# A two-block transformer kernel on one core: seven instead of five FFN slab pairs by the seven-product scheme

## The reference

```
h   = rmsnorm(x, ffn_norm_g)                      # 256 x 2048
hid = h @ w_ffn_in                                # 2048 -> 2 * 5632
x   = x + (silu(hid[:, :5632]) * hid[:, 5632:]) @ w_ffn_out   # 5632 -> 2048
x   = x + sigmoid(rmsnorm(x, ple_norm_g) @ w_ple_gate) * (p @ w_ple)
```

## Time and profile before

| | |
|---|---|
| median of 3 runs | 2035.05 us (2034.72 to 2035.17) |
| the profiled execution's own time | 2034.51 us |
| its span in the trace | 2032.8 us |
| TensorE busy | 2016.9 us (99%) |
| VectorE busy | 1406.7 us (69%) |
| ScalarE busy | 1049.3 us (52%) |
| granted TensorE clock | 1.00 throughout |
| HBM read | 384.46 MB, 190 GB/s over the span |

### The profile page before, as it was taken

How to read it: one execution, slowest core, us unless ns; L and a number is a source line. 1 busy time by engine, 2 the same in 40 slices (tenths; PEclk the granted TensorE clock), 3 DMA queues, 4 the chain that set the end, 5 groups by cost and what they waited for, 6 DMA issues and landing times.

```text
span 2032.8 us, 23614 instructions
## 1 busy us (share of the span) xinstructions
PE 2016.9 (99%) x9325; PEld 1677.2 (83%) x9325; DVE 1406.7 (69%) x1488; ACT 1049.3 (52%) x1309; POOL 34.0 (2%) x44
## 2 busy tenths in 40 slices
PE   8999999999999999999999999999999999999999
PEld 7888888888888888888888887888888888888787
DVE  6877676555666665655554557888878888888764
ACT  6545444554465556544444445555555555555453
POOL 1000000000001100000000000000000000000000
PEclk9999999999999999999999999999999999999999
DMA  8545354555556544555555556676666756665553
GB/s 283 167 144 166 124 187 149 196 186 201 194 186 208 174 165 143 187 184 188 186 191 195 186 187 212 195 241 206 217 210 214 238 196 217 209 215 200 176 183 124
DMA packets 197721, 387.98 MB, mean 191 GB/s; under 512 B 9282, under 2 KB 10996, under 8 KB 197492
## 3 DMA queue, kind: packets, MB, share of 16 engines
q1 hardware_dynamic: 197620, 386.59, 56.9%
HBM read 384.46 MB, written 2.10 MB: 190 GB/s over the span
## 4 chain that ended last, share of the span: by engine, by line
PE 96%; DVE 2%; ACT 1%; issue 1%; DMA 0%; SPq 0%; ACTq 0%; DVEq 0%
PE acc L1099 54%; PE acc L1104 27%; PE aux L1498 6%; PE aux L1502 3%; PE aux L1082 2%; PE aux L1163 1%; DVE wlo L1588 1%; PE aux L1519 0%; ACT whi L709 0%; DMA resid<-in_x 0%; DVE actB_lo L2327 0%; DVE act_whole L2309 0%; PE aux L1153 0%; PE aux L1178 0%; DVE att_z L2088 0%
## 5 line engine op out<-in xcount | busy, mean ns | idle before, releaser
L1588 DVE TENSOR_TENSOR wlo<-raw,whi 128x1024 fp32r<-128x1024 f32 x624 | 761.3, 1224 | 542.8 <-ACT whi L709 537.6
L709 ACT ACTIVATE whi<-raw 128x1024 fp32r<-128x1024 f32 x624 | 659.1, 1060 | 863.9 <-PE acc L1104 810.8
L1099 PE MATMUL acc<-whi,actA_hi 128*128 128x512 f32 x1152 | 454.6, 395 | 1.7 <-DVE actA_lo L1603 1.2
L1099 PE MATMUL acc<-whi,actA_lo 128*128 128x512 f32 x1152 | 449.5, 390 | 0.0
L1099 PE MATMUL acc<-whi,actB_hi 128*128 128x512 f32 x828 | 324.7, 392 | 0.0
L1099 PE MATMUL acc<-whi,actB_lo 128*128 128x512 f32 x828 | 322.3, 389 | 0.0
L1104 PE MATMUL acc<-wlo,actA_hi 128*128 128x512 f32 x1152 | 308.5, 390 | 0.5 <-DVE wlo L1588 0.5
L1099 PEld LDWEIGHTS acc<-whi,actA_hi 128*128 128x128 f32 x1152 | 216.9, 188 | 47.0 <-DVE actA_lo L1603 1.6
L1104 PEld LDWEIGHTS acc<-wlo,actA_hi 128*128 128x128 f32 x1152 | 216.3, 188 | 46.2 <-DVE wlo L1588 0.9
L1099 PEld LDWEIGHTS acc<-whi,actA_lo 128*128 128x128 f32 x1152 | 217.0, 188 | 43.8
L1104 PE MATMUL acc<-wlo,actB_hi 128*128 128x512 f32 x828 | 221.8, 390 | 0.7 <-DVE wlo L1588 0.6
(11 more groups left out here) (313 smaller groups left out, 1997.2 us busy)
## 6 DMA issues: line engine op xcount, KB each, us to landing
raw<-in_w_in SPq DMA_DIRECT2D x132, 1024.0 KB, 5.0
raw<-in_w_ffn_in SPq DMA_DIRECT2D x48, 1024.0 KB, 5.0
raw<-in_w_ffn_out SPq DMA_DIRECT2D x44, 1024.0 KB, 4.9
raw<-in_w_ffn_in SPq DMA_DIRECT2D x80, 512.0 KB, 4.5
raw<-in_w_out SPq DMA_DIRECT2D x16, 1024.0 KB, 4.9
raw<-in_w_pg SPq DMA_DIRECT2D x16, 1024.0 KB, 5.0
raw<-in_w_o SPq DMA_DIRECT2D x16, 1024.0 KB, 5.0
raw<-in_w_ple_gate SPq DMA_DIRECT2D x16, 1024.0 KB, 4.9
```

Of the source, the lines that this page charges most:

```text
L709: act.activation(whi[:, g % RING], raw_piece(g), ACT.Copy).then_inc(hi_ready, 1)
L1099: pe.matmul(acc2(n)[:, t, :], act[x][:, k + c, t * P:(t + 1) * P], whi[:, g % RING, c, :], start=(p == 0 and c == 0 and x == 0), stop=False)
L1588: dve.tensor_tensor(wlo[:, g % RING], raw_piece(g), whi[:, g % RING].bitcast(F32), ALU.subtract)\
```

## The change

Slabs 1, 2, 4, 5, 7, 8 and 10 go by the seven-product scheme, 0, 3, 6 and 9 in the standard way. Each of the seven blocks has two units of 8 standard pieces (BLOCKS) around its 28 s-pieces. The order of the products becomes M1, M2, M5, then M6/M7/M3 in turn, then M4; b21 is loaded twice (as b21 for M2 and as b21x for M4's sum). Out products go for two hidden slabs together (K = 1024): an out slab has 4 pieces, two slabs are open at a time, and out_added runs once for the two. Weight sums stay on VectorE, as they are. `fill` may use bank 2 or the bank opposite to the one of M1 (FILLS: block, standard piece after which it stands, hidden slab, half, bank). fill_hi and fill_lo stand at g + 3 instead of g + 4. The up half is summed in a step of its own (`s_up`, at M2's last piece + 3). The tail has 60 pieces: 4, out of slabs 9 and 8 together (16), out of 10 (8), and the gate (32). SBUF tensors are placed anew to make room. The diff, cut:

```diff
@@ -79,9 +79,24 @@
 ATT_START = (35, 55)
 
 
-S_GROUPS = 5
-S_ORDER = [("M1", q) for q in range(4)] + [("M5", q) for q in range(4)] + [(m, q) for q in range(4) for m in ("M6", "M7", "M3")] \
-    + [("M4", 0), ("M4", 1), ("M2", 0), ("M4", 2), ("M2", 1), ("M4", 3), ("M2", 2), ("M2", 3)]
+BLOCKS = [
+    (1, [("gate", 3), ("up", 3)]),
+    (2, [("gate", 6), ("out", (0, 1), 0)]),
+    (4, [("out", (0, 1), 2), ("up", 6)]),
+    (5, [("out", (3, 2), 0), ("out", (3, 2), 2)]),
+    (7, [("out", (6, 4), 0), ("out", (6, 4), 2)]),
+    (8, [("gate", 9), ("up", 9)]),
+    (10, [("out", (5, 7), 0), ("out", (5, 7), 2)]),
+]
+FILLS = [(0, 2, 0, 0, "d"), (0, 5, 0, 1, "d"), (1, 2, 1, 0, "d"), (1, 5, 1, 1, "d"), (2, 3, 3, 0, "d"), (2, 6, 3, 1, "d"),
+         (2, 8, 2, 0, "e"), (2, 11, 2, 1, "e"), (3, 11, 6, 0, "e"), (3, 14, 6, 1, "e"), (4, 0, 4, 0, "d"), (4, 3, 4, 1, "d"),
+         (4, 11, 5, 0, "e"), (4, 14, 5, 1, "e"), (5, 2, 7, 0, "d"), (5, 5, 7, 1, "d"), (6, 11, 9, 0, "e"), (6, 14, 9, 1, "e"),
+         (7, 0, 8, 0, "d"), (7, 3, 8, 1, "d"), (7, 6, 10, 0, "d"), (7, 9, 10, 1, "d")]
+HID_T = {0: 0, 1: 1, 2: 1, 3: 0, 4: 1, 5: 0, 6: 0, 7: 1, 8: 1, 9: 0, 10: 2}
+OUT_TAIL = ((9, 8), 10)
+S_GROUPS = len(BLOCKS)
+S_ORDER = [(m, q) for m in ("M1", "M2", "M5") for q in range(4)] + [(m, q) for q in range(4) for m in ("M6", "M7", "M3")] \
+    + [("M4", q) for q in range(4)]
 S_LEAD = 2
...
+    def unit(self, role, j, q=0):
+
+        if role == "out":
+            return [(role, j, q + i, p) for h in range(2) for i in range(2) for p in (2 * h, 2 * h + 1)]
+        return [(role, j, q, p) for p in range(8)]
 
...
-        for c, std in enumerate(blocks):
+        for c, (_, units) in enumerate(BLOCKS):
+            std = [x for u in units for x in self.unit(*u)]
             done = 0
             for t, x in enumerate(std):
+                self.after[c, t] = self.g
                 self.add_std(x, 2)
-                upto = max(0, min(28, (t - 1) * 28 // (len(std) - 4)))
+                upto = max(0, min(28, (t - 1) * 28 // (len(std) - 3)))
                 while done < upto:
                     self.add_s(c, done)
                     done += 1
             assert done == 28
...
+        pair, last = OUT_TAIL
+        tail = [("ple", 0, q, 0) for q in range(4)] + self.unit("out", pair, 0) + self.unit("out", pair, 2) \
+            + [("out1", last, q, p) for q in range(4) for p in range(2)]
...
@@ -201,10 +206,11 @@
                 free = self.s_at[c - 1, "M4", 2 * h + 1] if c else self.g_ffn + 10
                 self.loads.append((free, self.s_at[c, "M1", 2 * h], "r1", h, c))
             for i, (m, q) in enumerate(S_ORDER):
-                for what, first, last in (("b12", "M5", "M5"), ("b22", "M6", "M3"), ("b12x", "M7", "M7"), ("b21", "M4", "M2")):
+                for what, first, last in (("b21", "M2", "M2"), ("b12", "M5", "M5"), ("b22", "M6", "M3"), ("b12x", "M7", "M7"),
+                                          ("b21x", "M4", "M4")):
                     if m == first:
                         slot = RAW // 2 + n % 4
-                        need = at(i - S_LEAD)
+                        need = at(i if m == "M2" else i - S_LEAD)
                         self.loads.append((self.last_use[slot], need, "half", slot, (c, what, q)))
                         self.half[c, what, q] = (slot, 16 * (n // 4 + 1))
                         self.last_use[slot] = self.s_at[c, last, q]
...
-        S_BANK = {"M1": 0, "M6": 0, "M5": 1, "M3": 1, "M2": 1, "M7": 2, "M4": 3}
+        S_BANK = {"M5": 1, "M3": 1, "M7": 2}
         S_FORM = {"M5": 0, "M6": 1, "M7": 2, "M3": 3}
 
         def half_slot(c, what, q):
...
+        FILL_AT = [PLAN.after[c, t] for c, t, *_ in FILLS]
+        STD_J = [j for j in range(HIDDEN) if j not in [b[0] for b in BLOCKS]]
+
...
+        def own(c):
+
+            return 0 if c % 2 == 0 else 3
+
+        def s_bank(c, m):
+
+            b = S_BANK[m] if m in S_BANK else 3 - own(c) if m == "M2" else own(c)
+            return aux[:, b, :]
+
+        def filled(eng, j, h):
+
+            eng.wait_ge(sem("tr_taken"), 1 + [x[2:4] for x in FILLS].index((j, h)))
+
+        def fill_bank(f):
+
+            c, _, _, _, b = FILLS[f]
+            return aux[:, 2 if b == "d" else 3 - own(c), :].rearrange("p (c s) -> p c s", c=2)
+
...
                     if g == slab_end("gate", j) + 4:
-                        act.wait_ge(sem("hid_ready"), j // 2)
+                        act.wait_ge(sem("hid_ready"), i)
                         gated(PLAN.ffn_slab["gate", j, 0], ACT.Silu, "ffn", gate[0])
+                for f, at in enumerate(FILL_AT):
+                    if g == at + 3:
+                        fill_hi(f)
...
@@ -1473,23 +1503,25 @@
                         pe.wait_ge(sem("forms_lo"), 1)
                     else:
                         pe.wait_ge(sem("s_second_row"), c)
-                if m == "M5" and q == 0:
+                        pe.wait_ge(sem("tr_taken"), sum(at < g for at in FILL_AT))
+                if m == "M2" and q == 0:
                     pe.wait_ge(sem("hid_odd_ready"), c)
+                    pe.wait_ge(sem("tr_taken"), sum(at < g for at in FILL_AT))
+                if m == "M5" and q == 0 and c > 0:
+                    pe.wait_ge(sem("s_first_row"), c)
                 if m == "M6" and q == 0:
                     pe.wait_ge(sem("s_first"), c + 1)
                 if m == "M3" and q == 0:
                     pe.wait_ge(sem("s_fifth"), c + 1)
+                o = s_bank(c, m)
+                if m == "M7" and q == 0:
+                    pe.wait_ge(sem("tr_taken"), sum(at < g for at in FILL_AT))
                 if m == "M4" and q == 0:
-                    pe.wait_ge(sem("tr_taken"), FILLS.index(("even", c, 1)) + 1)
-                if m == "M2" and q == 0:
-                    pe.wait_ge(sem("s_first_row"), c + 1)
-                o = aux[:, S_BANK[m], :]
-
...
 
-            def fill(kind, c, h):
-
-                f = FILLS.index((kind, c, h))
-                if kind == "odd":
-                    pe.wait_ge(sem("hid_odd_ready"), c)
+            def fill(f):
+
+                c, _, j, h, b = FILLS[f]
+                if j in S_J:
+                    pe.wait_ge(sem("hid_odd_ready"), S_J.index(j) + 1)
+                    src = hid_s[S_J.index(j) % 2]
                 else:
-                    pe.wait_ge(sem("hid_ready"), c + 1)
+                    pe.wait_ge(sem("hid_ready"), STD_J.index(j) + 1)
+                    src = hid_std
                 if f == 0:
-                    aux_taken(pe, AUX[("hH", 7)] - (AUX[("hH", 7)] - 3) % 4)
-                pe.wait_ge(sem("tr_taken"), f) if f > 0 else None
-                src = hid_o if kind == "odd" else hid_e
+                    for i in range(4, 8):
+                        aux_taken(pe, AUX[("hH", i)])
+                else:
+                    pe.wait_ge(sem("tr_taken"), f)
+                if b == "e":
+                    pe.wait_ge(sem("s_up"), c + 1)
+                elif c > 0:
+                    pe.wait_ge(sem("s_second_row"), c)
                 for i in range(2):
                     for t in range(T):
-                        ins = pe.transpose(aux[:, 3, i * S + t * P:i * S + (t + 1) * P], src[:, t, (2 * h + i) * P:(2 * h + i + 1) * P],
...
+            def out_piece(n, role, j, q, p):
+
+                if role == "out1":
+                    if q == 0:
+                        filled(pe, j, p)
+                    piece(n, p, hidT[HID_T[j]], p * PK, p == 1)
+                else:
+                    if q == 0:
+                        filled(pe, j[p // 2], p % 2)
+                    piece(n, p, hidT[HID_T[j[p // 2]]], p % 2 * PK, p == 3)
 
             for kind, g, *x in PLAN.ffn:
...
+
+                dve.wait_ge(sem("tr_hi"), f + 1)
+                dve.tensor_tensor(fill_dst(1, f), fill_bank(f), fill_dst(0, f).bitcast(F32), ALU.subtract).then_inc(sem("tr_taken"), 1)
+
+            def s_up(c):
+
+                dve.wait_ge(sem("s_first"), c + 1)
+                s_done(dve, c, "M2")
+                x = hid_s[c % 2][:, 0, :]
+                dve.tensor_tensor(x, x, s_bank(c, "M2"), ALU.add).then_inc(sem("s_up"), 1)
 
...
             def s_hidden(c):
 
+                s_done(dve, c, "M4")
+                dve.wait_ge(sem("s_up"), c + 1)
+                h = hid_s[c % 2]
+                link(dve.tensor_tensor(h[:, 1, :], h[:, 1, :], s_bank(c, "M4"), ALU.add))
                 dve.wait_ge(sem("s_gate"), c + 1)
-                dve.wait_ge(sem("s_first"), c + 1)
...
@@ -2355,6 +2400,27 @@
                 slab_made(dve, n)
                 x = resid[:, :, q * COLS:(q + 1) * COLS]
                 dve.tensor_tensor(x, x, acc2(n), ALU.add).then_inc(acc_free[n % 2], 1)
+
+            def between(g):
+
+                for i, j in enumerate(STD_J):
+                    if g == slab_end("gate", j) + 4:
+                        gate_taken(PLAN.ffn_slab["gate", j, 0])
+                    if g == slab_end("up", j) + 3:
```

(79 more changed lines are left out.)

227 lines of the change are left out of this document (84 added, 143 removed).

## The result

The changed kernel took 2105.72 us (median of 4 runs, 2102.94 to 2106.61), the kernel before 2034.93: a ratio of 1.0341, 95% interval 1.0329 to 1.0353. The forecast was 2071, slower, with a range of 2046 to 2098. The sign was right and so were most of the places of the loss; the growth forecast, 36 us, was half of what came.

A forecast was written before the change was run, and what follows sets the result against it. TensorE was taken to bound the FFN, with VectorE close behind. Stalls of 8.6 + 16.6 + 14 + 7.7 = 46.9 us, less 10.9 saved, gave 36.0 us more: 2071 us, range 2046 to 2098.

The forecast's parts named there:

- What TensorE saves: Two more slab pairs as 168 matmuls instead of 192: 10.9 us less on TensorE.
- VectorE keeps up on the average: Per block, VectorE needs 77 to 80 us against TensorE's 81.6, so it fits at 94 to 98% load.
- Fills ahead of M1: Blocks 0, 1 and 5: M1 waits for the fills before it, idling TensorE 1.6, 3.7 and 3.3 us, sum 8.6.
- The second pair: At t2 of blocks 1 to 6: late pair load or accumulator, 1.1 or 3.6 us each, sum 16.6.
- DMA bound: Rival, chance 0.12: bursts at block ends hold up r1 and M2's blocks too, giving 2090 to 2110 us.
- b21x: M4's third piece: its load has no piece between, so TensorE idles 2.0 us in each of seven blocks, 14.
- The dense middle: Around M5 and M7: VectorE's lead runs short, 4.2 us in block 2 and 3.5 in out-unit blocks, sum 7.7.
- kinds 2 and 3: Stalls at the second pair of each block (16.6 us) and at b21x for M4's third piece (14 us).
- kinds 1 and 4: Stalls at the fills ahead of M1 (8.6 us) and in the dense middle (7.7 us).
- a falling clock: Rival, chance 0.03: TensorE's clock drops to 1.2 GHz for 4 us after six boundary stalls, giving 2083 us.
- the rival's own price: Falling-clock rival, chance 0.03: half of 4 us lost behind each of six boundary stalls, 12 us more.
- The rival of DMA being at its rate: Rival, chance 0.12: DMA bursts at block ends hold up r1 and M2's blocks, 2090 to 2110 us.

The follow-up runs named there:

- e6: e4 with the 28 s-pieces of a block spread evenly over t1 to t15 and the fills moved along: 2026.90 us, ratio to before 0.9961.
- e3: Changed kernel with the fills ahead of M1 (blocks 0, 1, 5) and of M7 (block 2) one standard piece later: 2092.52 us.
- e1: Changed kernel where a half load takes the half place that falls free first instead of the next in turn: 2086.42 us.
- e7: Kernel before, with TensorE held at its five block ends while GpSimd does one small power operation: 2048.19 us.
- e8: Kernel before, with TensorE held at its five block ends while GpSimd does two small power operations: 2061.32 us.
- e4: Changed kernel with first-free half places, the t2/t3 pair loaded ahead of r1's second MB, and fills one standard piece later: 2055.18 us, ratio to before 1.0099.

## Why the prediction was wrong in size

**What TensorE saves: right in what the matmuls are worth.** e6 shows busy time 9.8 us lower, of 10.9. But "PE busy time falls by about 11 us" failed for the changed kernel itself, where it rose by 18.2: the forecast had no term for what a stall does to the matmuls behind it.

**VectorE keeps up on the average: right.** 94 to 98% were worked out; e6 runs at 93 to 96%, and its longest wait of TensorE in the blocks is 1.35 us. Average load was not the bound.

**1. Fills ahead of M1: 8.6 foreseen, 4.8 measured** (1.83 in block 1, 2.99 in block 5). In block 0 there was none: the added wait stands in the branch for later blocks, which I had read over. In block 0 the high part of the fill and M1's matmuls run side by side. e3, which moves M7's fill too, gave 13.2 us.

**2. The second pair: 16.6 foreseen, 24.2 measured**: 1.99, 6.29, 4.33, 2.40, 0.55 and 4.54 at the six block ends, and 4.13 at the entry to the tail, which I had not counted, though the same two-piece distance holds there. The failing term is the load: 5.0 us and "up to 2.7 more" for the MB in front, 7.7 in all. It was 8.4 to 10.8 us from issue to landing at the six block ends. In the stretch shown r1's first MB and three half loads, issued from 1435 us on, stood in front of it too. The median of the earlier trace rows, 5.0 us, is the price in a queue with gaps; after the change the queue was full just when it counted. I had put this case with the rivals ("DMA bound", 0.12), whose 2090 to 2110 held the time, but not for its reason alone.

**3. b21x: 14 foreseen, 21.5 measured**, in all seven blocks, mostly in two steps of 1.2 to 2.4 us: TensorE waits at t14 and again at M4's third piece; e1 took most of it away. VectorE waited 2.7 to 5.1 us for this load, 3.7 in the mean, where I had 2.3. The addition was off as well: 12.1 less 7.7, less a lead of 0.5 to 3, is 1.4 to 3.9 us and not the 1.2 to 2.7 written there. The 2.0 taken is near the low end; 3.1 per block was measured.

**4. The dense middle: 7.7 foreseen, 5.1 measured**; M7 behind its fill was 4.02 of 4.2.

The four make 55.6 us of stalls instead of 46.9. That the sums come so close is partly luck: kinds 2 and 3 are 15.1 us over the forecast, kinds 1 and 4 are 6.4 under it. Some 2 us of small waits of the kernel before are gone, so idle time grew by 53.5 us, 6.6 more than forecast. The span grew by 71.7 us instead of 36.0; of these 35.7 us more, 6.6 are idle time and 29.1 the matmuls that took longer.

**The step that failed: the forecast put what a stall does to the matmuls behind it at nothing, and it came to 29.1 us, 22.7 of them the clock.** The rest are, by the estimate above, the pauses. The prediction gave a falling clock a chance of 0.03, from the one row at hand: 3.1 us of idle at the start of the kernel with a granted clock of 1.00. That one stall was taken for a rule. Of e7's five stalls of 2 us one brought the clock down, of e8's five of 4 us four did. A single stall without a fall says little; a forecast of some fifteen stalls of 2 to 5 us should have counted their price as the stall and the lost clock behind it. The rule of the Trainium skill named there (TensorE: Matmul & The Clock Gate, Part 1) spoke for the fall, and the trace of after agrees with it; even the rival's own price, 12 us, was about half of what it cost. Which of the shorter stalls bring a fall the runs leave open.

The rival of DMA being at its rate is partly right: the rate is reached, but only in bursts at block ends, and e6 moves the same 403 MB with ScalarE waiting 4.5 us for a load at the most and hardly a wait of TensorE.

## What to carry to other kernels

A change that takes spare work away from between two loads should be judged by distances, not by shares: list for each load the piece that frees its place and the one that needs it, and compare the time between with a load's time in a full queue. Here two places in that list (no piece between, and two behind a burst) cost 45 us of stalls, and choosing the place that falls free first, the order of two loads, more room behind the fills and an even spread of the pieces turned a kernel 3.4% slower into one 0.4% faster. On TensorE a stall of 2 us or more may cost 1.7 or 3.4 us of clock behind it, up to as much again as the stall.

## What the runs showed of the hardware

The granted clock falls behind some stalls and not behind others of the same size: not behind the 2.41 us at 1439.31, but behind the 2.40 us at 1731.12 in the same run. All five stalls of the changed kernel of 4 us and more had one, and it had begun before four of them ended. In the changed kernel and e1 to e8 the lost clock was between 1.7 us (e6, e7) and 25.6 us, without what lies behind the last matmul. In four of these runs (e1 to e4) it also fell once near 304 us, in the first block, where no wait of TensorE is shown and nothing was changed. Just before stand twelve small matmuls with an operand of 4 rows (302.30 to 304.54 us in e4); the kernel before has them too, without a fall. e4, stretches of 4 us:

```profile
300.00:304.00 4.00, 4.00 (x22) 3.15 (x21) 1.67 (x2) 1.86 (x2) 0.00 (x0) 1.00 0.75 248
304.00:308.00 4.00, 4.00 (x12) 2.90 (x11) 3.96 (x10) 0.00 (x0) 0.00 (x0) 0.57 0.53 164
```

That costs 1.7 us, and its cause stays open; whether it is part of why the kernel before spread from 2033.9 to 2037.2 us is not shown.
